# A hybrid decoder layer: the delta rule's chunk matrices stored 64 columns wide, the first stage's units in another order, and the last expert's weights in single transfers

## Chip, cores and metric

The kernel is written in Bass and runs on one core of a Trainium2 chip. The metric is device time in microseconds (us); lower is better. TensorE is called PE, VectorE DVE, ScalarE ACT, GpSimd POOL and SyncE SP.

## What is computed

One layer over 256 tokens of width 1024, in float32. A token mixer has three branches (a gated delta rule with 4 heads of 128, a short gated convolution, and cross-attention into 256 memory tokens), then comes a mixture of 32 experts, 4 to a token, of inner width 1024. Only the delta rule's part within a chunk of 64 tokens is touched in its arithmetic:

```
decay  = exp(where(causal, g_cum_i - g_cum_j, -inf))          # 64 x 64 for each head and chunk
kk     = where(strict, (k*beta) @ k.T * decay, 0)
u, kc  = solve(kk + I, [v*beta, k*beta*exp(g_cum)])            # unit lower triangular
qk     = q @ k.T * decay
step c:  v_new = u - kc @ S;  o = q_dec @ S + qk @ v_new;  S = S*cd + k_end.T @ v_new
```

## The kernel before, in words

**Units and their order.** `mixer_schedule` (lines 100 to 160) writes out one list of units by hand, and every engine walks through that list in order: a unit is, for instance, ("qkv", n), 128 columns of the input projection (24 products of three split float32r operands, L1159 to L1161), ("km", n) and ("vm", t) the memory's keys and values, ("memT", n) and ("hT", t, j) the turning of memory and of the normalised tokens, ("ab", 0) and ("abT", 0) the eight columns of decay and beta, and ("g", name) a step of the delta rule. Units take three PSUM banks in turn (0 to 2): PE waits until the bank of three units ago is free. Weights arrive in slots of 2 MB and are split in pieces (`prep`): ACT rounds the high part (L1035), DVE or POOL subtracts it for the low part (L738). Piece q+3 comes ahead of the unit that uses piece q, and ACT waits for the end of the use of piece q before it writes piece q+3. `vm` takes pieces 4 to 7 (`project_rows`, both tiles of tokens in one run of products), `qkv` n takes piece 8+n.

**The delta rule.** Two chunks of 64 tokens lie on the 128 partitions of a tile, so there are 8 pairs p of tile and head (NPB = 8). Before, each of the matrices LT, LTs, T1, X, XT and decayT is 128x128 for a pair, with only the two diagonal 64x64 blocks other than zero. The steps `scores`, `lx0`, and from n = 1 to 5 `lx n` and `xlx n` build the inverse of the triangular matrix level by level; `xlx` 1 to 4 have two sets of eight products, `xlx5` one. POOL cuts the level's part out of LT by a mask (L978), ACT copies T1 (L466), DVE subtracts (L668 to L683). `kcum`, then `vnew c` and `state c` for the chunks c = 0 to 3, go over the chunks. Between two steps of the delta rule stands mostly one projection unit.

**Masks.** POOL writes the constants at the start (`masks`, L935 to L959) and only then its first low part (L738).

**Experts.** Each expert has 6 chunks of 2 MB: four of gate and up, two of down. They go to a ring of 10 slots. From expert 7 on SP sends the gate and up chunks in pairs of 4 MB (L882 to L894); a pair waits until both slots are free, and signals once. `chunk_spent` is SP's wait for PE's use.

**Barriers.** `ln` at line 1537 waits for tokens and for both LayerNorm parameters before the first statistics.

## Time and profile before

| | |
|---|---|
| median of 3 runs (lowest, highest) | 1306.23 us (1304.66, 1307.99) |
| the profiled execution's own time | 1307.05 us |
| its span, first to last instruction | 1305.3 us |
| mean granted clock of PE, share of full speed | 0.988 |
| bytes moved by DMA | 453.59 MB, 347 GB/s over the span |

The profile comes from one execution; its own time is 1.75 us longer than its span. A row of a timeline gives the start from the beginning of the span, the length, the engine and line, the operation, what it writes and reads, its shape and how many instructions are merged in the row; in brackets stands for how long the engine was idle before and what ended that. PEld is PE's weight load. A float32 product is issued as two instructions, so that "x16" on PE is 8 products. A form such as 128*64 is the part of the array that the weights take, rows and columns: 64*64 is a quarter of it. L numbers are lines of the kernel before.

### The profile page before, as it was taken

What the parts mean: (1) busy time and instruction counts of PE and PEld (TensorE: products, weight loads), DVE (VectorE), ACT (ScalarE), POOL (GpSimd) and SP (SyncE); (2) the same over time, 40 slices, a digit from 0 to 9 for tenths busy, and PEclk for the clock granted to TensorE, in tenths of its full rate; (3) what the DMA queues carried; (4) which work ended last, traced back from release to release, by engine and by line L of the source; (5) the groups of instructions that cost most, each with busy time, mean ns of one, the idle gap of its engine ahead of it and who ended that gap; (6) DMA issues with size and microseconds to landing.
All of it is one profiled execution on the core that took longest, in us unless ns stands there. A gap on an engine that the chain in (4) does not pass through costs nothing.

```text
span 1305.3 us, 16418 instructions
## 1 busy us (share of the span) xinstructions
PE 1236.5 (95%) x6871; PEld 631.9 (48%) x6871; DVE 403.7 (31%) x794; ACT 241.5 (18%) x387; POOL 146.4 (11%) x102
## 2 busy tenths in 40 slices
PE   5899999999999999999999999999999999999996
PEld 5699899899763333333333333333333333323332
DVE  5484563333541222212212212221212222121214
ACT  4453344344321000000000001000000000000001
POOL 6232432355400000000000000000000000000000
PEclk9899999999999999999999999999999999999998
DMA  9443231195499999999999999999999999999993
GB/s 309 141 169 130 79 116 66 65 382 207 160 388 423 398 418 428 424 429 429 430 427 429 433 430 430 431 431 433 426 428 430 433 432 427 430 429 432 427 428 142
DMA packets 49222, 453.59 MB, mean 347 GB/s; under 512 B 6078, under 2 KB 10251, under 8 KB 30987
## 3 DMA queue, kind: packets, MB, share of 16 engines
q1 hardware_dynamic: 49162, 452.71, 83.8%
q8 instruction: 49, 0.80, 0.3%
q14 instruction: 11, 0.08, 0.0%
HBM read 451.64 MB, written 1.05 MB: 347 GB/s over the span
## 4 chain that ended last, share of the span: by engine, by line
PE 70%; DMA 22%; DVE 4%; ACT 2%; issue 1%; SPq 1%; POOL 0%; DVEq 0%; ACTq 0%
PE bank L1339 25%; DMA late<-in_w_gate_up_dram 16%; PE bank L1412 12%; PE bank L1159 6%; PE bank L1160 5%; PE bank L1161 5%; DMA raw<-in_w_gate_up_dram 5%; PE bank L1425 3%; PE bank L1310 3%; PE bank L1325 2%; PE bank L1400 1%; ACT late L1131 1%; PE bank L549 1%; PE bank L554 1%; DMA early<-in_ln_b_dram 1%
## 5 line engine op out<-in xcount | busy, mean ns | idle before, releaser
L1339 PE MATMUL bank<-late 128*64 128x512 f32 x1632 | 366.6, 596 | 14.3 <-DMA late<-in_w_gate_up_dram 14.3
L1339 PEld LDWEIGHTS bank<-late 128*64 128x64 f32 x1632 | 112.0, 137 | 245.8 <-issue 213.8
L1412 PE MATMUL bank<-late 128*64 128x512 f32 x816 | 182.5, 599 | 5.3 <-ACT late L1131 5.3
L1159 PE MATMUL bank<-act_hi,w_hi 128*128 128x256 f32 x448 | 129.6, 289 | 1.7 <-DVE early L1610 1.3
L1160 PE MATMUL bank<-act_lo,w_hi 128*128 128x256 f32 x448 | 126.6, 283 | 0.0
L1161 PE MATMUL bank<-act_hi,w_lo 128*128 128x256 f32 x448 | 126.4, 282 | 0.0
L1753 DVE TENSOR_SCALAR late<-bank 128x512 f32<-128x512 f32 x32 | 22.1, 692 | 308.5 <-PE bank L1339 308.5
L1412 PEld LDWEIGHTS bank<-late 128*64 128x64 f32 x816 | 56.9, 138 | 112.8 <-issue 104.4
L1339 PE MATMUL bank<-raw,late 128*64 128x512 f32 x416 | 93.4, 596 | 3.5 <-DMA raw<-in_w_gate_up_dram 3.5
L738 POOL TENSOR_TENSOR w_lo<-raw,w_hi 128x1024 fp32r<-128x1024 f32 x33 | 80.4, 2438 | 131.7 <-ACT w_hi L1035 131.6
L1159 PEld LDWEIGHTS bank<-act_hi,w_hi 128*128 128x128 f32 x448 | 85.1, 190 | 3.4 <-DVE early L1610 1.5
L1160 PEld LDWEIGHTS bank<-act_lo,w_hi 128*128 128x128 f32 x448 | 85.2, 190 | 0.1
L1161 PEld LDWEIGHTS bank<-act_hi,w_lo 128*128 128x128 f32 x448 | 85.2, 190 | 0.0
L1764 DVE COPY late<-bank 64x512 f32<-64x512 f32 x32 | 22.2, 694 | 190.0 <-PE bank L1412 190.0
L1124 ACT COPY late<-bank 128x512 f32<-128x512 f32 x33 | 19.3, 586 | 332.5 <-PE bank L1310 332.5
L1035 ACT CAST w_hi<-raw 128x1024 fp32r<-128x1024 f32 x56 | 58.5, 1047 | 80.8 <-issue 54.0
L1425 PE MATMUL bank<-late 64*128 64x512 f32 x256 | 63.6, 615 | 1.0 <-DVE late L1824 1.0
L1310 PE MATMUL bank<-hx,late 128*64 128x512 f32 x264 | 62.3, 593 | 0.0
L1133 ACT COPY late<-bank 64x512 f32<-64x512 f32 x32 | 18.5, 579 | 232.0 <-PE bank L1412 232.0
L1339 PEld LDWEIGHTS bank<-raw,late 128*64 128x64 f32 x416 | 28.6, 137 | 62.8 <-issue 55.8
L1129 ACT ACTIVATE late<-late 128x512 f32<-128x512 f32 x32 | 20.1, 629 | 182.7 <-DVE late L1753 182.7
L1768 DVE COPY late<-bank 128x256 f32<-128x256 f32 x31 | 13.2, 425 | 131.2 <-PE bank L1420 131.2
(318 smaller groups left out, 1306.1 us busy)
## 6 DMA issues: line engine op xcount, KB each, us to landing
late<-in_w_gate_up_dram SPq DMA_DIRECT2D x40, 4096.0 KB, 32.5
late<-in_w_down_dram SPq DMA_DIRECT2D x51, 2048.0 KB, 31.1
late<-in_w_gate_up_dram SPq DMA_DIRECT2D x22, 2048.0 KB, 13.4
raw<-in_w_gate_up_dram SPq DMA_DIRECT2D x10, 4096.0 KB, 32.6
raw<-in_w_down_dram SPq DMA_DIRECT2D x13, 2048.0 KB, 33.1
raw<-in_w_in_dram SPq DMA_DIRECT2D x8, 2048.0 KB, 8.4
early<-in_w_in_dram SPq DMA_DIRECT2D x6, 2048.0 KB, 7.9
raw<-in_w_gate_up_dram SPq DMA_DIRECT2D x6, 2048.0 KB, 10.3
```

Source lines behind the costliest of these rows:

```text
L738: ops.tensor_tensor(lo, src, as_f32(hi), ALU.subtract).then_inc(split_lo[who], 1)
L1035: a.copy(hi, src).then_inc(split_hi, 1)
L1159: mm(o, l_hi, r_hi, start=start, stop=False)
L1160: mm(o, l_hi, r_lo, start=False, stop=False)
L1161: return mm(o, l_lo, r_hi, start=False, stop=stop)
L1310: ins = mm(ps[0][64 * c:64 * c + 64, :], onehot[:, t, :], hx[:, t, 512 * c:512 * (c + 1)], start=(t == 0), stop=(t == NT - 1))
L1325: mm(ps[1 + n][64 * c:64 * c + 64, :], e_row[rows, :], bgu[rows, :], start=True, stop=False)
L1339: ins = mm(bk[64 * c:64 * c + 64, :], x_slotT[:, k % 4, 64 * (k // 4):64 * (k // 4) + 64], w[:, kk, at + 512 * c:at + 512 * (c + 1)], star ...
L1412: ins = mm(ps[3][64 * c:64 * c + 64, :], hidT[:, kk, 64 * q:64 * q + 64], w[:, kk, c * 512:(c + 1) * 512], start=(q == 0 and kk == 0), sto ...
L1425: ins = mm(ps[4 + 2 * t + c][:, :], scatter[64 * c:64 * c + 64, t * P:(t + 1) * P], y_tok[64 * c:64 * c + 64, :], start=False, stop=True, ...
L1753: d.tensor_scalar(gate1, ps[1][:, :], LIMIT, None, ALU.min).then_inc(gate_cut, 1)
L1764: d.tensor_copy(y_tok[64:128, :], ps[3][64:128, :]).then_inc(y_copied, 1)
```

## The change

The matrices of the delta rule are stored as two stacked 64x64 blocks, 64 columns wide (`T1`, `LTs`, `X`, `XT`, new `LTc` and `decayTc`). Each product of a pair becomes two, one for each 64 rows (`CHUNK_ROWS`); those of `lx` and `xlx` read partitions 0 to 63 or 64 to 127 and write the same partitions of one bank. `lx0` is now a product with the identity in place of a transpose, `norms` multiplies by 128 columns of ones in place of one, and ACT reads its results from four banks. The copies of ACT, DVE and POOL on these matrices cover half the columns. In the list of units, `vm` now stands between the turns of token tile 0 and of tile 1, `ab`, `abT` and `log decay` stand among the `qkv` units, and `decay` between qkv 9 and 10. The turn of the small parameters (`cols`) is a step of its own, between km 2 and 3. POOL gets four more copies at the end of the masks. The first LayerNorm's statistics no longer wait for its parameters. SP sends the last expert's gate and up chunks one by one. The diff, its context left out (`out_c(b, rows, p)` is the slice `ps[b][rows, p*64:(p+1)*64]`):

```diff
@@ -104,11 +104,11 @@
-    order += [("km", 0), ("ln", 0, 1), ("km", 1), ("km", 2), ("km", 3)]
-    order += [("hT", t, j) for t in range(NT) for j in range(2)] + [("ab", 0), ("abT", 0), ("log decay",)]
-    order += [("vm", n) for n in range(NT)]
-    order += [("g", "scalars"), ("qkv", 0), ("qkv", 1), ("g", "decay"), ("qkv", 2)]
-    order += [("qkv", n) for n in range(3, 12)]
+    order += [("km", 0), ("ln", 0, 1), ("km", 1), ("km", 2), ("cols",), ("km", 3)]
+    order += [("hT", 0, j) for j in range(2)] + [("vm", n) for n in range(NT)] + [("hT", 1, j) for j in range(2)]
+    order += [("qkv", 0), ("qkv", 1), ("ab", 0), ("qkv", 2), ("abT", 0), ("qkv", 3), ("log decay",)]
+    order += [("qkv", n) for n in range(4, 8)] + [("g", "scalars"), ("qkv", 8), ("qkv", 9), ("g", "decay")]
+    order += [("qkv", 10), ("qkv", 11)]
...
@@ -238,7 +238,7 @@
-        T1, LTs = e.at(o_pad, NPB, P), [e.at(o_pad + R, NPB, P), e.at(o_pad + 2 * R, NPB, P)]
+        T1, LTs = e.at(o_pad, NPB, CHUNK), [e.at(o_pad + R, NPB, CHUNK), e.at(o_pad + 2 * R, NPB, CHUNK)]
...
@@ -258,7 +258,7 @@
-        o_x = e.used; X, XT = e.new(NPB, P), e.new(NPB, P)
+        o_x = e.used; X, XT, LTc, decayTc = (e.new(NPB, CHUNK) for _ in range(4))
...
@@ -268,7 +268,9 @@
-        w_ab, ab_rows = e.at(o_qkv + R, KD, 2 * H), e.at(o_qkv, T)
+        w_ab, ab_rows = e.at(o_qkv + R, KD, 2 * H), e.at(o_eb, T)
+        chunk_ident = sb("chunk_ident", [P, CHUNK], scope=early)
+        chunk_mask = sb("chunk_mask", [P, LEVELS, CHUNK], BF16, early)
...
@@ -450,8 +455,11 @@
-                a.activation(inv_norm.rearrange("p t h -> p (t h)"), ps[4][:, 0:2 * NPB], ACT.Sqrt,
-                             bias=eps_rms[:, 0:1]).then_inc(g_act, 1)
+                for t in range(NT):
+                    for n in range(2):
+                        ins = a.activation(inv_norm[:, t, 4 * n:4 * n + 4], ps[4 + 2 * t + n][:, 0::P], ACT.Sqrt,
+                                           bias=eps_rms[:, 0:1])
+                ins.then_inc(g_act, 1)
...
@@ -462,13 +470,12 @@
-                for n in range(2):
-                    ins = a.copy(T1[:, H * n:H * n + H, :].rearrange("p a b -> p (a b)"), ps[4 + n][:, :])
-                ins.then_inc(g_act, 1)
+                a.copy(T1.rearrange("p a b -> p (a b)"), ps[4][:, :]).then_inc(g_act, 1)
-                for n in range(2):
-                    ins = a.mul(nkcT_of(n), ps[4 + n][:, :].rearrange("p (a b) -> p a b", b=P), -1.0)
+                for s, rows in enumerate(CHUNK_ROWS):
+                    ins = a.mul(nkcT.rearrange("p h (t n) -> p t h n", t=NT)[:, :, :, rows],
+                                ps[4 + s][:, :].rearrange("p (t h n) -> p t h n", t=NT, h=H), -1.0)
...
@@ -516,8 +523,7 @@
-                        ins = mm(ps[4][:, t * 2 * H + n:t * 2 * H + n + 1], squares[:, n, t * P:(t + 1) * P], ones[:, 0:1],
-                                 start=True, stop=True)
+                        ins = mm(out4(t * 2 * H + n), squares[:, n, t * P:(t + 1) * P], ones[:], start=True, stop=True)
...
@@ -528,9 +534,11 @@
-                    mm(out4(p), chunk_T(kT, p), chunk_T(kT, p), start=True, stop=True)
+                    for rows in CHUNK_ROWS:
+                        mm(out_c(4, rows, p), chunk_T(kT, p)[:, rows], chunk_T(kT, p)[:, rows], start=True, stop=True)
-                    ins = mm(out4(NPB + p), chunk_T(kT, p), chunk_T(qT, p), start=True, stop=True)
+                    for rows in CHUNK_ROWS:
+                        ins = mm(out_c(6, rows, p), chunk_T(kT, p)[:, rows], chunk_T(qT, p)[:, rows], start=True, stop=True)
...
@@ -543,22 +551,24 @@
-                    if n == 0:
-                        ins = tr(out4(p), LTs[0][:, p, :], ident[:])
-                    else:
-                        ins = mm(out4(p), LTs[n % 2][:, p, :], X[:, p, :], start=True, stop=True)
+                    for rows in CHUNK_ROWS:
+                        ins = mm(out_c(4, rows, p), LTs[n % 2][rows, p, :], ident[rows, rows] if n == 0 else X[rows, p, :],
+                                 start=True, stop=True)
-                    ins = mm(out4(p), T1[:, p, :], XT[:, p, :], start=True, stop=True)
+                    for rows in CHUNK_ROWS:
+                        ins = mm(out_c(4, rows, p), T1[rows, p, :], XT[rows, p, :], start=True, stop=True)
-                        ins = mm(out4(NPB + p), XT[:, p, :], T1[:, p, :], start=True, stop=True)
+                        for rows in CHUNK_ROWS:
+                            ins = mm(out_c(6, rows, p), XT[rows, p, :], T1[rows, p, :], start=True, stop=True)
-                    ins = mm(out4(p), kbe[:, p, :], XT[:, p, :], start=True, stop=True)
+                    for s, rows in enumerate(CHUNK_ROWS):
+                        ins = mm(out_c(4 + s, slice(0, P), p), kbe[rows, p, :], XT[rows, p, :], start=True, stop=True)
...
@@ -567,7 +577,8 @@
-                    ins = mm(o, XT[:, t * H + h, lo:lo + CHUNK], vbeta[:, t * H + h, :], start=True, stop=(c == 0))
+                    rows = CHUNK_ROWS[c % 2]
+                    ins = mm(o, XT[rows, t * H + h, :], vbeta[rows, t * H + h, :], start=True, stop=(c == 0))
...
@@ -637,13 +648,12 @@
-                step(d.tensor_tensor(LT, LT, decayT, ALU.mult))
-                for n in range(2):
-                    o = flat(LT[:, H * n:H * n + H, :])
-                    step(d.tensor_tensor(o, o, ps[4 + n][:, :], ALU.mult))
-                for n in range(2):
-                    o = flat(decayT[:, H * n:H * n + H, :])
-                    step(d.tensor_tensor(o, o, ps[6 + n][:, :], ALU.mult))
+                for rows in CHUNK_ROWS:
+                    step(d.tensor_tensor(LTc[rows], LT[rows, :, rows], ps[4][rows, :].rearrange("p (a n) -> p a n", a=NPB), ALU.mult))
+                for rows in CHUNK_ROWS:
+                    step(d.tensor_tensor(LTc[rows], LTc[rows], decayT[rows, :, rows], ALU.mult))
+                for rows in CHUNK_ROWS:
+                    d.tensor_tensor(decayTc[rows], decayT[rows, :, rows], ps[6][rows, :].rearrange("p (a n) -> p a n", a=NPB), ALU.mult)
...
@@ -667,20 +677,13 @@
-                for n in range(2):
-                    ins = d.tensor_tensor(X[:, H * n:H * n + H, :], ident_8[:, 0:H, :],
-                                          ps[4 + n][:, :].rearrange("p (a n) -> p a n", a=H), ALU.subtract)
-                ins.then_inc(g_dve, 1)
+                d.tensor_tensor(X, ident_8, ps[4][:, :].rearrange("p (a n) -> p a n", a=NPB), ALU.subtract).then_inc(g_dve, 1)
-                for n in range(2):
-                    o = flat(XT[:, H * n:H * n + H, :])
-                    ins = d.tensor_tensor(o, o, ps[4 + n][:, :], ALU.subtract)
+                ins = d.tensor_tensor(flat(XT), flat(XT), ps[4][:, :], ALU.subtract)
-                    for n in range(2):
-                        o = flat(X[:, H * n:H * n + H, :])
-                        ins = d.tensor_tensor(o, o, ps[6 + n][:, :], ALU.subtract)
+                    ins = d.tensor_tensor(flat(X), flat(X), ps[6][:, :], ALU.subtract)
...
@@ -786,7 +789,7 @@
-            return m < PAIRED_FROM or m % 2 == 0 or m % EC == EC - 1
+            return m < PAIRED_FROM or m >= (NE - 1) * EC or m % 2 == 0 or m % EC == EC - 1
...
@@ -879,7 +882,7 @@
-            with sp.Fori(1, ROUNDS) as j:
+            with sp.Fori(1, ROUNDS - 1) as j:
@@ -892,6 +895,18 @@
+            for ex in range(2 + ROUND * (ROUNDS - 1), NE):
+                paired = ex < NE - 1
+                for c in range(EC):
+                    m = EC * ex + c
+                    if c < 4 and paired:
+                        if c % 2 == 0:
+                            chunk_spent(sp, m + 2 - RING)
+                            pair_dma(sp, c, w_gate_up[0, ex], m)
+                    else:
+                        chunk_spent(sp, m + 1 - RING)
+                        chunk_dma(sp, c, w_gate_up[0, ex], w_down[0, ex], *ring_place(m)[0:2])
...
@@ -956,7 +971,14 @@
+                step(ins)
+                for rows in CHUNK_ROWS:
+                    step(eng.tensor_copy(chunk_ident[rows, :], ident[rows, rows]))
+                    ins = eng.tensor_copy(chunk_mask[rows, :, :], level_mask[rows, :, rows])
+                    if rows.start == 0:
+                        step(ins)
+                pool.wait_ge(consts, 3)
...
@@ -974,8 +996,8 @@
-                    m = level_mask[:, n:n + 1, :].broadcast_to([P, NPB, P])
-                    eng.tensor_tensor(LTs[n % 2], LT, m, ALU.mult).then_inc(g_pool, 1)
+                    m = chunk_mask[:, n:n + 1, :].broadcast_to([P, NPB, CHUNK])
+                    eng.tensor_tensor(LTs[n % 2], LTc, m, ALU.mult).then_inc(g_pool, 1)
...
@@ -1207,6 +1229,9 @@
+                if kind == "cols":
+                    pe.wait_ge(rows_in, 80)
+                    tr(ps[3][:, 0:N_ROWS], small_rows[:, :], ident[0:N_ROWS, 0:N_ROWS]).then_inc(cols_turned, 1)
@@ -1237,8 +1262,6 @@
-                    pe.wait_ge(rows_in, 80)
-                    tr(ps[3][:, 0:N_ROWS], small_rows[:, :], ident[0:N_ROWS, 0:N_ROWS]).then_inc(cols_turned, 1)
...
@@ -1251,6 +1274,8 @@
+                    if s == ("qkv", 0):
+                        wait_copied(pe, "hT", 4)
...
@@ -1536,10 +1561,10 @@
-                            v.wait_ge(lnp_in[0], 32)
+                        v.wait_ge(lnp_in[0], 32)
```

## Rows read from the trace of the kernel before

**Rows 1.** The page, busy time of each engine over the whole span.
```profile
PE 1236.5 (95%) x6871; PEld 631.9 (48%) x6871; DVE 403.7 (31%) x794; ACT 241.5 (18%) x387; POOL 146.4 (11%) x102
```
**Rows 2.** Busy time by stretch: engines, granted clock, share of DMA time, GB/s.
```profile
28.10:55.60 27.50, 19.41 (x92) 14.31 (x93) 13.87 (x22) 12.57 (x19) 7.97 (x3) 0.81 0.46 165
...
32.40:42.60 10.20, 5.14 (x24) 3.34 (x25) 5.46 (x8) 2.46 (x3) 1.41 (x1) 0.50 0.47 173
...
107.40:110.90 3.50, 3.50 (x18) 3.50 (x18) 0.25 (x1) 0.28 (x1) 0.00 (x0) 0.51 0.73 275
...
135.00:205.30 70.30, 66.59 (x557) 65.43 (x556) 42.64 (x70) 27.34 (x50) 26.42 (x12) 1.00 0.25 91
...
254.00:382.00 128.00, 124.07 (x918) 115.83 (x916) 60.21 (x130) 52.37 (x80) 54.28 (x30) 0.97 0.68 261
382.00:830.00 448.00, 442.84 (x2104) 151.60 (x2102) 100.32 (x208) 39.37 (x65) 0.00 (x0) 1.00 1.00 424
830.00:1260.00 430.00, 409.00 (x1952) 139.75 (x1950) 94.93 (x202) 35.13 (x59) 0.00 (x0) 1.00 1.00 430
```
**Rows 3.** Timeline of TensorE, first stage: start, length, instructions, idle time before and its releaser.
```profile
20.92 0.36 PE L1159 MATMUL bank<-src_hi,w_hi 128*128 128x256 f32 x1 [1.29 <-POOL w_lo L738]
...
35.99 1.12 PE L1237 MATMUL bank<-ident,hx 128*128 128x128 f32 x4 [3.61 <-DVE act_lo L1601]
...
44.28 0.50 PE L1159 MATMUL bank<-w_hi,src_hi 128*128 128x512 f32 x1
...
55.58 0.28 PE L504 MATMUL bank<-tiny,block_upper 128*128 128x8 f32 x2
```
**Rows 4.** The same timeline for GpSimd, ScalarE and VectorE, first stage.
```profile
13.70 3.15 POOL L955 TENSOR_TENSOR level_mask<-early 128x128 bf16<-128x128 f32 x6
...
18.40 2.37 POOL L738 TENSOR_TENSOR w_lo<-raw,w_hi 128x1024 fp32r<-128x1024 f32 x1
...
27.04 1.05 ACT L1035 CAST w_hi<-raw 128x1024 fp32r<-128x1024 f32 x1 [0.26 <-DMA raw<-in_w_mem_kv_dram]
...
47.38 1.28 ACT L1059 ACT_TABLE_LOAD   x1
...
56.78 1.07 ACT L1047 COPY early<-bank 128x512 f32<-128x512 f32 x2
...
37.76 0.69 DVE L1601 TENSOR_TENSOR act_lo<-bank,act_hi 128x512 fp32r<-128x512 f32 x1 [0.64 <-ACT act_hi L1040]
```
**Rows 5.** The chain of waits, the delta rule's steps: start, length, what.
```profile
103.96 3.46 PE bank L519 x32
...
146.89 1.78 PE bank L554 x16
```
**Rows 6.** Timeline of TensorE, the same stage: two steps that found it waiting.
```profile
136.15 1.09 PE L547 MATMUL bank<-ident,early 128*128 128x128 f32 x8 [1.08 <-POOL early L978]
...
142.04 2.02 PE L549 MATMUL bank<-early 128*128 128x128 f32 x16 [1.97 <-issue]
```
**Rows 7.** Timeline of the weight loads, steps over the chunks: one pair of loads a row.
```profile
216.36 0.25 PEld L570 LDWEIGHTS bank<-early 128*64 128x64 f32 x2
216.58 0.25 PEld L572 LDWEIGHTS bank<-early 128*64 128x64 f32 x2
...
221.34 0.19 PEld L583 LDWEIGHTS bank<-early 128*64 128x64 f32 x2 [0.17 <-issue]
221.70 0.19 PEld L584 LDWEIGHTS bank<-early 64*64 64x64 f32 x2 [0.17 <-issue]
```
**Rows 8.** Timeline of the weight loads, an expert's biases and what follows them.
```profile
409.84 0.21 PEld L1325 LDWEIGHTS bank<-late 32*64 32x64 f32 x8 [0.81 <-issue]
410.86 0.14 PEld L1339 LDWEIGHTS bank<-late 128*64 128x64 f32 x2 [0.81 <-issue]
```
**Rows 9.** Timeline of TensorE, the last expert's first products by each pair of chunks.
```profile
1262.92 3.65 PE L1339 MATMUL bank<-late 128*64 128x512 f32 x16 [1.03 <-DMA late<-in_w_gate_up_dram]
...
1273.69 7.09 PE L1339 MATMUL bank<-late 128*64 128x512 f32 x32 [1.45 <-DMA late<-in_w_gate_up_dram]
```

More of the change, by code:

```diff
@@ L163 @@
 SCHEDULE, PIECES_OF = mixer_schedule()
-NOT_UNITS = ("g", "prep", "ln", "ya", "sum hi", "sum", "soft", "log decay")
+NOT_UNITS = ("g", "prep", "ln", "ya", "sum hi", "sum", "soft", "log decay", "cols")
 UNITS = [s for s in SCHEDULE if s[0] not in NOT_UNITS]
@@ L438, in hybrid_layer @@
             GD[name] = gd
+        CHUNK_ROWS = [slice(CHUNK * n, CHUNK * (n + 1)) for n in range(P // CHUNK)]
         def act_gdn(act, name):
@@ L480, in act_gdn @@
                 a.activation(o_rs, o_ss, ACT.Sqrt, bias=eps_rms[:, 0:1], scale=1.0 / DH).then_inc(g_act, 1)
-        def nkcT_of(t):
-            return nkcT[:, :, t * P:(t + 1) * P]
         def pt4(h):
@@ L495, in spread, with out_c @@
                 return a[:, t, n:n + 1].broadcast_to([P, P])
+            def out_c(b, rows, p):
+                return ps[b][rows, p * CHUNK:(p + 1) * CHUNK]
             def chunk_T(a, p):
@@ L583, in pe_gdn @@
                         mm(o, qT[:, h, t * P + lo:t * P + lo + CHUNK], state[:, h, :], start=True, stop=False)
-                    mm(o, decayT[rows, t * H + h, rows], vnew[rows, h, :], start=(c == 0), stop=True)
+                    mm(o, decayTc[rows, t * H + h, :], vnew[rows, h, :], start=(c == 0), stop=True)
                 for h in range(H):
@@ L601, in flat @@
                 return a.rearrange("p a b -> p (a b)")
-            ident_8 = ident[:].rearrange("p (a n) -> p a n", a=1).broadcast_to([P, NPB, P])
+            ident_8 = chunk_ident[:].rearrange("p (a n) -> p a n", a=1).broadcast_to([P, NPB, CHUNK])
             if name == "scalars":
@@ L1577, in _ @@
                                     ALU.subtract).then_inc(bank_free[bank_of(u)], 1)
+                    continue
+                if kind == "cols":
+                    v.wait_ge(cols_turned, 1)
+                    d.tensor_copy(small_cols[:], ps[3][:, 0:N_ROWS]).then_inc(cols_ready, 1)
+                    v.wait_ge(cols_ready, 1)
                     continue
@@ L1618, in _ @@
                 elif kind == "ab":
-                    v.wait_ge(cols_turned, 1)
-                    d.tensor_copy(small_cols[:], ps[3][:, 0:N_ROWS]).then_inc(cols_ready, 1)
-                    v.wait_ge(cols_ready, 1)
                     full()
```

## Prediction

> **What bounds the kernel now.** The page comes first: PE is busy 95% of the span [rows 1]. Then the stretches. From 382 us on the experts run with DMA at its full share and 424 to 430 GB/s, PE nearly always busy up to 830 us and waiting 21 us of 430 after that [rows 2]: the stream of weights sets the pace there, PE just behind it. Ahead of that DMA is far from full (share 0.68 even in the last stretch of the mixer, 0.25 in the delta rule's) and PE is the bound: 124.07 of 128 us busy, 66.59 of 70.3 [rows 2]. The stream of expert weights starts when the mixer frees its slots, so what the mixer saves on PE should move all that follows. The first stage stands out: from 28.1 to 55.6 us PE is busy 19.41 of 27.5 us, at half clock from 32.4 to 42.6 [rows 2].
>
> All sums are made against the profiled execution's own time, 1307.05 us; the median is 0.8 us lower. About 0.3% (4 us) is what a measurement here can tell from no change.
>
> **First stage.** Before, the last turn of a token tile waits 3.61 us for DVE's queue, `ab` follows at half clock, and `vm` runs only from 44.28 to 55.58, 11.3 us; then qkv 0 starts, 55.9 [rows 3]. After, I lay it out anew:
> - POOL gets five more waits and four copies of 64 rows, two of 64 and two of 384 columns, ahead of its first low part. The nearest row has 0.525 us for 128 columns with two inputs (3.15 for six) [rows 4]: 3.7 us at that price, half of it if a copy with one input costs half. I take 2.6, towards the middle. The low part that ends at 20.77 and releases PE at 20.92 [rows 3, 4] then comes at 23.5; two km units of 24 products at 0.118 us (11.3 us for 48 longer ones is twice that) bring 29.3. The statistics, freed of the parameters, only shorten DVE's side.
> - Two turns end at about 30.5. The high part of piece 4 still starts at 27.04, since its DMA lands then; 1.05 us of ACT and 2.37 of POOL [rows 4] give 30.5 too. `vm` ends at 42.
> - Then a new hole. ACT's order is the copy for piece 10 (which waits for the end of `vm`), both copies of `vm`, then the high parts of token tile 1: 1.05 + 1.07 + two of about 0.6, then DVE's 0.69 [rows 4], 4.0 us. qkv 0 needs all four turns and starts at 46.
> - `ab`, `abT` and `scalars` now stand behind that: 24 products of 0.118 us and 0.5, 3.4 us, so the comparable time is 49.4. ACT's three table loads of 1.28 us each for `abT` [rows 4] had `vm` as cover; now they stand among silus and high parts that are ordered only three pieces ahead. They hold ACT for 4.5 us where two units of 2.85 us less 3.4 us for a piece give slack of 2.3: about 1.7 us of wait, 51.1.
> - Clock: holes of 4 us stand where PE waits for POOL and behind `vm`. It fell once at such a place before; a shorter spell lasted 3.5 us at 0.51 [rows 2], 1.7 us lost. One and a half such losses: 53.6.
>
> Gain 55.9 - 53.6 = **2.3 us**; between -1.5 (both holes cold, POOL at full price) and 5.5 (no cold spell, cheap copies). The moved `decay` has the same neighbours in kind (two qkv units) as before: nothing either way. `cols` on PE is one small turn, and it goes in the wait on the parts of km.
>
> **Norms.** 16 one-column products take 3.46 us [rows 5]; 16 full ones take 3.56 (two sets of 1.78). Behind them the clock was 0.51 for 3.5 us [rows 2], with PE busy all the time, which costs 1.7 us. If columns that work keep it up, that returns; from 0 to 1.7, I take 1.5, as nothing else stands before that fall. ACT's four reads in place of one hide behind a unit.
>
> **The delta rule's products.** A set of eight 128x128 products takes 1.78 us, 0.111 for each of 16 instructions [rows 5]. There are 18 sets: scores 2, lx0 1 (transposes, 0.9 us), lx 5, xlx 9, kcum 1: 17 x 1.78 + 0.9 = 31.2 us. After, each set is 32 instructions of half the columns in weights and in what streams, 0.056 us each. The question is whether the two blocks run side by side. An expert's biases answer it: eight instructions of 512 columns (0.44 us each alone, by 0.111 for 128) in four places of the array take 1.02 us from first load to the next stage's first [rows 8], not 3.6. So a set takes 16 x 0.056 = 0.9. Each change of the array's form costs: pairs of one form follow each other in 0.22 us, pairs of alternating forms in 0.36 [rows 7], 0.145 for a change. Before, these steps had none, after two each (projections are 128*128). Seven single sets 1.19 each, five double (scores, xlx 1 to 4) 2.09, kcum with 128 weight columns 1.78 + 0.29: 8.3 + 10.4 + 2.1 = 20.8. **Gain 10.4 us**; if the blocks don't overlap, none and 5 us of cost (below).
>
> `vnew` 1 to 3 get worse: the product with XT is now 64*64 and the next 128*64, which is just what `state` has; 0.36 in place of 0.22 a pair, 8 pairs, three times: **3.5 us lost**. `vnew0` and `state` stay.
>
> **Waits in that stage.** 66.59 of 70.3 us busy leaves 3.7 idle [rows 2], of which lx0 waits 1.08 for POOL's mask product and lx1 1.97 [rows 6], behind DVE's X. Both operands are halved in columns, each of three copies from over 2 us to about 1.1, while PE's own steps shorten by 0.6 to 1.5 beside units of 2.85. I take 2.8 of the 3.7; bounds 1 and 3.7.
>
> **The last expert.** PE waits 1.03 us for the first pair of chunks and 1.45 for the second [rows 9]. A chunk is half a pair, 4.9 us at 430 GB/s [rows 2]; sent singly the first half lands that much earlier, so both waits go and the second half is there when it is needed: **2.5 us**. Below, 0 if the last down chunks are late instead (they must land by 1285); above, 3.5. SP issues two more transfers, far ahead of a stream 36 us deep, at no cost.
>
> Sum: 2.3 + 1.5 + 10.4 - 3.5 + 2.8 + 2.5 = 16.0. 1307.05 - 16.0 = 1291.0, and 1290.2 for the median.
>
> **A rule against the change.** The biases' first two row tiles write one bank at the same time, in different halves of its partitions, and still all eight end in 1.02 us; one bank at a time would take 1.8 [rows 8]. The Trainium skill, TensorEngine Tiling (Array Packing), section Restrictions and Gotchas, says that "Different row tiles cannot access same PSUM bank simultaneously". By it the blocks of lx and xlx, which share a bank, would run one behind the other, and the sum would be 2.5. The trace disagrees with the rule for different partitions, and the sum goes by the trace.
>
> **Rivals.**
> - *Blocks of one bank take turns*: 64-row blocks might behave otherwise than the biases' 32-row ones. Seven sets cost 0.9 us more and four double ones 1.8: 13.5 us, 1303.7. The page above is the rule for it; rows 8 speak against it. 12%.
> - *A change of place costs like a change of form*, at lx, xlx, scores and kcum: every one of 288 products then stands alone, 0.111 + 0.145 in place of 0.056, 58 us more, 1348. It turns into a loss from 0.056 us a product over the forecast. Rows 8 speak against it (the place changes there at no cost), no row shows it for short products. 4%.
> - *The first stage loses*: POOL's copies at full price, both holes cold, ACT's tables holding pieces back longer: -2 in place of 2.3, 1294.5. For it, the hole behind `vm` is sure; against it, `vm` no longer waits for `ab`. 14%.
> - *The mixer's gain is swallowed by the weights*: if their stream didn't start earlier, only the end's 2.5 us would stay, 1303.7. Against it, share 0.68 ahead of 382 us. 4%.
> - The forecast has 66%, its own range 1284 to 1300 by the bounds above.
>
> The range goes from 1284 to 1304, which takes in the two cases at 1303.7. Faster by over 0.3% is the forecast and the third rival, 0.80; within 0.3% the first and the fourth, 0.14 of their 0.16; slower 0.06, the second and what the others may add.
>
> **What would show it.** Right: lx and xlx sets at 0.9 us with 0.15 idle ahead of them, `vnew` pairs at 0.36 apart, no half clock behind norms, no waits at lx0 and lx1, a hole of 4 us behind `vm`, and no wait ahead of the last expert's third chunk. Wrong: sets at 1.8 us or more (the blocks take turns), qkv 0 later than 49 us, or a mixer that ends 13 us earlier with experts that end less so.

## The result, and the profile after

| | median, us | runs |
|---|---|---|
| kernel before | 1305.89 | 1304.66 to 1307.99 (4) |
| kernel after | 1297.25 | 1295.85 to 1298.25 (4) |

The ratio is 0.9931 with the interval 0.9914 to 0.9949: faster by 8.6 us. The forecast was 16.0 us, 1290.2. The profiled execution of after took 1295.85 us with a span of 1294.0; by the two profiled executions the difference is 11.2 us.

The page of the kernel after, busy time of each engine and the granted clock in 40 slices:

```profile
PE 1226.6 (95%) x7167; PEld 618.8 (48%) x7167; DVE 392.9 (30%) x785; ACT 240.3 (19%) x386; POOL 144.9 (11%) x106
...
PEclk8999999999999999999999999999999999999998
```

PE is 9.9 us less busy than in [rows 1]. Where that went is read from marks that both kernels have. Each row is a start time in the two profiles, from the chain of waits, which has the norms 0.16 us later than TensorE's timeline, and the last column is what the stretch up to it gained (+) or lost (-):

| mark | before | after | stretch |
|---|---|---|---|
| qkv 0 | 55.94 | 50.78 | |
| norms | 103.96 | 108.00 | -4.04 (from the start) |
| scores | 121.14 | 123.66 | +1.5 |
| lx0 | 136.15 | 136.96 | +1.7 |
| vnew0 | 205.56 | 196.73 | +9.6 |
| end of state3 | 252.27 | 246.42 | -3.0 |
| `down` of the expert before the last | 1253.78 | 1245.23 | +2.7 |
| last `down` | 1284.14 | 1272.81 | +2.8 |

Of the 2.7 us between state3 and the experts' end, 1.5 are a spell of half clock at 401 us in the profile of before; after has none there. The medians are 8.64 us apart, 2.7 less than the marks say. That the marks at the end of state3 and at the last expert give 5.85 and 2.8, 8.65 together, fits, but no run shows that the 2.7 us are missing in the other executions.

**The delta rule's products.** The chain of waits of after, its steps from the scores to kcum (start, length, what):

```profile
123.66 1.08 PE bank L538 x32
...
136.96 1.15 PE bank L555 x32
...
145.25 1.08 PE bank L562 x32
...
190.46 1.93 PE bank L571 x32
```

A set that took 1.78 us in 16 instructions [rows 5] now takes 1.08 in 32. The second set of a double step takes 0.93 (146.33 to 147.26), and kcum 1.93. So the two blocks of 64 rows run at the same time although they write one bank. The start times of the single instructions say the same: in the set at 141.14 the two blocks' instructions start 0.007 us apart, and the next two 0.058 us after the first two.

**The steps over the chunks.** The weight loads of after, one pair of loads a row:

```profile
207.15 0.19 PEld L581 LDWEIGHTS bank<-early 64*64 64x64 f32 x2 [0.33 <-issue]
207.51 0.19 PEld L583 LDWEIGHTS bank<-early 128*64 128x64 f32 x2 [0.17 <-issue]
```

The pairs of `vnew` stand 0.36 us apart, as those of `state` did before [rows 7].

**The first stage.** TensorE's timeline of after; in brackets the idle time ahead of the row and its releaser:

```profile
25.46 0.55 PE L1181 MATMUL bank<-src_hi,w_hi 128*128 128x256 f32 x1 [5.60 <-POOL w_lo L741]
...
35.23 0.47 PE L1181 MATMUL bank<-w_hi,src_hi 128*128 128x512 f32 x1 [0.67 <-ACT early L1067]
...
68.19 0.39 PE L1181 MATMUL bank<-act_hi,w_hi 128*128 128x256 f32 x1 [1.15 <-DVE early L1640]
...
76.05 0.36 PE L1181 MATMUL bank<-act_hi,w_hi 128*128 128x256 f32 x1 [1.92 <-POOL w_lo L741]
...
79.40 0.39 PE L1181 MATMUL bank<-act_hi,w_hi 128*128 128x256 f32 x1 [0.28 <-DVE early L1640]
...
107.84 3.73 PE L526 MATMUL bank<-ones,early 128*128 128x128 f32 x32
```

The waits of 1.15, 1.92 and 0.28 us have two causes. ScalarE and VectorE ahead of them:

```profile
63.88 1.05 ACT L1057 CAST w_hi<-raw 128x1024 fp32r<-128x1024 f32 x1 [2.80 <-issue]
...
71.03 1.28 ACT L1081 ACT_TABLE_LOAD   x1
```

```profile
64.97 1.23 DVE L741 TENSOR_TENSOR w_lo<-raw,w_hi 128x1024 fp32r<-128x1024 f32 x1 [2.98 <-ACT w_hi L1057]
66.11 0.48 DVE L1637 TENSOR_SCALAR early<-bank,small_cols 128x256 f32<-128x256 f32 x1
```

The 1.92 and 0.28 us come behind the table loads of `abT` (65.27, 69.51 and 71.03) and the one back to silu (73.49): the high parts that they wait for start only at 72.44 and 75.11. The 1.15 us at 68.19 have no table load ahead of them in their chain. ACT stood idle for 2.80 us before it, since a piece may be overwritten only when PE is done with it; DVE stood behind that high part, read the bank of `qkv` 2 only from 66.11 on, and PE, with the short unit `abT` between, was back at that bank before DVE had read it.

The low part that released PE at 20.92 [rows 3] now does so at 25.46. GpSimd's timeline says why:

```profile
18.48 0.23 POOL L976 COPY chunk_ident<-ident 64x64 f32<-64x64 f32 x1
18.77 0.50 POOL L977 COPY chunk_mask<-level_mask 64x384 bf16<-64x384 bf16 x1
19.33 1.11 POOL L976 COPY chunk_ident<-ident 64x64 f32<-64x64 f32 x1
20.51 1.53 POOL L977 COPY chunk_mask<-level_mask 64x384 bf16<-64x384 bf16 x1
22.12 3.19 POOL L741 TENSOR_TENSOR w_lo<-raw,w_hi 128x1024 fp32r<-128x1024 f32 x1
```

The first two copies take 0.73 us, and the same two for the other rows 2.64; the low part takes 3.19 instead of 2.37 [rows 4]. What differs is the neighbour and not the rows: put off to 110.97 us (experiment 1), the same copies take 1.23 and 0.54 us for the first rows and 0.23 and 0.51 for the others, and there VectorE's low part ends at 112.11. VectorE at the start of after:

```profile
18.84 1.51 DVE L1530 SCALAR_TENSOR_TENSOR hx<-hx,tiny,early 128x1024 f32<-128x1024 f32 x1
20.38 1.28 DVE L1532 SCALAR_TENSOR_TENSOR hx<-hx,tiny,early 128x1024 f32<-128x1024 f32 x1
21.70 1.41 DVE L741 TENSOR_TENSOR w_lo<-raw,w_hi 128x1024 fp32r<-128x1024 f32 x1
```

These read two tensors each and run back to back from 18.84 on. The first of them started at 21.01 in the kernel before; the statistics, rid of the parameters, came early enough to meet POOL's copies.

Busy time by stretch of the kernel after (window, its length, PE, PEld, DVE, ACT, POOL, then granted clock, share of DMA time and GB/s):

```profile
23.60:30.40 6.80, 4.94 (x23) 4.97 (x24) 4.17 (x8) 1.61 (x3) 3.74 (x2) 0.50 1.05 395
...
46.50:50.78 4.28, 1.26 (x9) 0.81 (x8) 1.29 (x2) 2.99 (x5) 2.35 (x1) 1.00 0.29 107
...
50.86:54.28 3.42, 3.42 (x17) 3.42 (x18) 0.00 (x0) 0.00 (x0) 0.00 (x0) 0.50 0.00 0
...
111.50:115.00 3.50, 3.50 (x32) 3.50 (x31) 0.26 (x1) 1.24 (x5) 0.00 (x0) 1.00 1.01 383
...
135.80:196.60 60.80, 58.36 (x824) 55.21 (x822) 34.60 (x60) 25.17 (x46) 21.26 (x12) 1.00 0.30 105
```

The clock is at its lower level, 1.2 GHz, three times before the norms: from 13.30 to 16.70 in the first unit of km (0.50 too, and the wait for POOL covers it), at the third unit of km, behind the wait of 5.60 us, and at qkv 0, behind the hole of 4.28 us. Behind the norms it stays at 2.4 GHz where it had fallen before [rows 2].

**The last expert.** TensorE's timeline of after:

```profile
1253.26 3.65 PE L1364 MATMUL bank<-late 128*64 128x512 f32 x16
...
1262.41 7.04 PE L1364 MATMUL bank<-late 128*64 128x512 f32 x32
...
1272.81 7.09 PE L1437 MATMUL bank<-raw,late 128*64 128x512 f32 x32 [0.27 <-ACT late L1153]
```

Nothing waits for a chunk of `gate_up` any more, where 1.03 and 1.45 us stood [rows 9].

### The profile page after: what moved, and what is told of

It reads as the page before. It is cut to its first block, busy times and chain, and to the rows that moved or that the text cites. A ratio compares the mean times of both kernels' runs of the same rounds, so it can differ in the third digit from the quotient of the medians.

```text
span 1294.0 us, 16946 instructions
## 1 busy us (share of the span) xinstructions
PE 1226.6 (95%) x7167; PEld 618.8 (48%) x7167; DVE 392.9 (30%) x785; ACT 240.3 (19%) x386; POOL 144.9 (11%) x106
## 4 chain that ended last, share of the span: by engine, by line
PE 69%; DMA 21%; DVE 3%; ACT 2%; issue 1%; POOL 0%; SPq 0%; DVEq 0%; ACTq 0%
PE bank L1364 25%; DMA late<-in_w_gate_up_dram 21%; PE bank L1437 12%; PE bank L1181 6%; PE bank L1182 5%; PE bank L1183 5%; PE bank L1450 3%; PE bank L1335 3%; PE bank L1350 2%; PE bank L1425 1%; ACT late L1153 1%; ACT w_hi L1057 1%; PE bank L1445 1%; PE bank L555 1%; PE bank L562 0%
## 6 DMA issues: line engine op xcount, KB each, us to landing
late<-in_w_down_dram SPq DMA_DIRECT2D x51, 2048.0 KB, 31.3
```

## The experiments

All times are medians, each beside runs of the kernel before on the same chip (1306 to 1308 us). The ratios come from all the runs, not from the two medians, so they differ a little from those medians' quotient. A difference from the kernel after is one of medians and crosses chips; differences under 2 us between two variants are not told apart here.

**1. POOL's copies put off.** The four copies go out of the start and run at the norms.

```
-                for rows in CHUNK_ROWS:
-                    step(eng.tensor_copy(chunk_ident[rows, :], ident[rows, rows]))
-                    ins = eng.tensor_copy(chunk_mask[rows, :, :], level_mask[rows, :, rows])
...
+                if s == ("g", "norms"):
+                    for rows in CHUNK_ROWS:
+                        step(eng.tensor_copy(chunk_ident[rows, :], ident[rows, rows]))
+                        step(eng.tensor_copy(chunk_mask[rows, :, :], level_mask[rows, :, rows]))
```

> The changed kernel with one thing moved: GpSimd's four new copies (the two diagonal blocks of the identity and of the level masks) stand at the norms step instead of at the end of the masks, so that its first low part of a weight piece comes as early as before. Nothing is left out. My theory: in the changed kernel those copies and the low part behind them, slowed by VectorE's two-input work, end at 25.4 us where before they ended at 20.8, and TensorE waits 5.6 us for them. Moved away, km 2 starts at about 21 us, vm at about 31 us instead of 35.2, and the whole gains 4 us: 1293 us, with the hole at 20 us down to about 1.3 us. Rival: vm is tied to the landing and split of its own pieces (the high part of piece 4 starts at 27.2 us in either kernel), so the hole only moves to before vm: gain under 1.5 us, 1296 or more.

Measured: 1296.85 us (1296.16 to 1298.31), ratio 0.9918 (0.989 to 0.9947). No gain over after. The copies did hold up km, whose third unit now starts at 21.20 instead of 25.46 and its fourth at 24.57 instead of 30.61, and all that came back was lost ten microseconds later: the norms start at 108.79, where after has 107.84. TensorE, VectorE and GpSimd of this kernel:

```profile
36.04 0.77 PE L1180 MATMUL bank<-w_hi,src_hi 128*128 128x512 f32 x1 [2.85 <-DVE act_lo L1630]
```

```profile
27.96 1.28 DVE L1531 SCALAR_TENSOR_TENSOR hx<-hx,tiny,early 128x1024 f32<-128x1024 f32 x1
29.28 2.23 DVE L1570 CAST w_ab_hi<-early 128x64 fp32r<-128x64 f32 x1
31.62 2.26 DVE L1571 TENSOR_TENSOR w_ab_lo<-early,w_ab_hi 128x64 fp32r<-128x64 f32 x1
33.80 1.21 DVE L741 TENSOR_TENSOR w_lo<-raw,w_hi 128x1024 fp32r<-128x1024 f32 x1
```

```profile
28.54 5.25 POOL L741 TENSOR_TENSOR w_lo<-raw,w_hi 128x1024 fp32r<-128x1024 f32 x2 [7.78 <-ACT w_hi L1056]
```

The split of `ab`'s 64 columns takes 0.20 us an operation in the kernel after, where POOL is idle at that time:

```profile
27.96 0.20 DVE L1571 CAST w_ab_hi<-early 128x64 fp32r<-128x64 f32 x1
```

Here it takes 2.23 and 2.26 while POOL works through two low parts, and `vm` waits for a low part of h queued behind it.

**2. The old order of the first stage**, the rest of the change kept: all four turns, `ab`, `vm`, qkv 0.

> The changed kernel with the order of units of the kernel before from hT on (both token tiles' turns, ab, abT and log decay ahead of vm, scalars and decay among the first qkv units). The new copies stay in their early place. Nothing is left out. My theory: the new order costs, it does not gain, since it opens a hole of 4 us behind vm and takes away the cover of ScalarE's three table loads; with the old order and the earlier statistics the turns end at about 36 us, vm at 52.5, norms starts at about 100 instead of 108, and the time is 1290 us. Rival: the new order saves the 8 us of half-idle TensorE that the old one has ahead of vm, and the lateness comes from the copies alone: 1300 us or more.

Measured: 1291.97 us (1290.02 to 1292.76), ratio 0.9878 (0.9849 to 0.9908), 5.3 us better than after. The norms start at 102.75 instead of 107.84. The new order costs about what TensorE's timeline says of the norms, 5.1 us, less than the 7 us expected. The wait for POOL's low part is still there (4.55 us at 25.57): it is not the order's.

**3. Both together.**

> Both edits together: old order of units and the four copies moved to the norms step. Nothing is left out. My theory: the two add up nearly; turns end at about 31 us, vm runs from 35 to 46.5, norms starts at about 95 us, the time is 1285 us (1283 to 1288). Rival: one hole covers the other, and it is no faster than the better of the two alone.

Measured: 1293.55 us (1292.02 to 1296.57), ratio 0.9899 (0.9867 to 0.9931). No better than the old order alone: the two operations of the split took 2.24 and 2.29 us, a turn waited 3.13 for DVE, and the clock was at half for 13.65 us from 30.8 on.

**4. The blocks apart.** All upper blocks of a set are issued before all lower ones; the work is the same. One of the five loops:

```
-                for p in range(NPB):
-                    for rows in CHUNK_ROWS:
+                for rows in CHUNK_ROWS:
+                    for p in range(NPB):
                         ins = mm(out_c(4, rows, p), T1[rows, p, :], XT[rows, p, :], start=True, stop=True)
```

> The changed kernel with the loops over pair and block exchanged in scores, lx and xlx: all eight products of partitions 0 to 63 first, then all eight of partitions 64 to 127. The same products, nothing is left out. My theory: two blocks overlap only when neighbours in the queue use different places of the array; apart, a set takes 32 x 0.056 = 1.8 us instead of the 0.93 to 1.08 measured, and 16 sets cost 0.8 us more each, less what lies in waits: 1308 to 1311 us. Rival: TensorE's queue looks far enough ahead, or starts the second block's products while the first block's run, and the set stays at about 1 us: 1297 us.

Measured: 1306.99 us (1304.83 to 1309.9, ten runs), ratio 1.0001 (0.9986 to 1.0016): 9.7 us above after, 1 us less than expected. Its chain of waits:

```profile
138.42 1.87 PE bank L555 x32
143.32 1.82 PE bank L555 x32
```

and its costliest groups between 120 and 210 us (count, busy time, mean ns of one, idle time before), with the same group of after below:

```profile
L555 PE MATMUL bank<-early 64*64 64x64 f32 x160 | 9.5, 221 | 0.0
```

```profile
L555 PE MATMUL bank<-early 64*64 64x64 f32 x160 | 5.7, 221 | 0.8 <-issue 0.8
```

One product takes 221 ns from start to end in both, and only the overlap differs. Two products' instructions side by side in the queue and in different places take 0.058 us together; instructions for one place behind each other start 0.058 us apart each, and the whole gain of the change is gone.

**5. Products grouped by form.** `vnew` and `state` issue all 64\*64 products of a chunk, then all 128\*64 ones. Each head's first product keeps its start mark. The Trainium skill, PSUM — Partial Sum Buffer, section The four PSUM rules, says that a second group's start in the same bank and rows makes the first group's next product overwrite its sum; so this kernel leaves the first part of the sums of heads 0 to 2 out of its output. It issues the same instructions.

```
                 for h in range(H):
...
-                    if c:
-                        ins = mm(o, nkcT[:, h, t * P + lo:t * P + lo + CHUNK], state[:, h, :], start=False, stop=True)
+                for h in range(H if c else 0):
+                    ins = mm(ps[6][rows, h * DH:(h + 1) * DH], nkcT[:, h, t * P + lo:t * P + lo + CHUNK], state[:, h, :],
+                             start=False, stop=True, skip_group_check=True)
```

> The changed kernel with the products of vnew and state regrouped: in vnew first the four heads' products with XT (64*64 part of the array), then the four with the state (128*64), in state first the four with the queries (128*64), then the four with decayTc (64*64); the sums in PSUM are the same. Nothing is left out. My theory: each change of the form costs 0.145 us and has no cover, so 6 changes fewer in each of six steps give 36 x 0.145 = 5.2 us: 1292 us, with rows of pairs 0.22 us apart. Rival: the gap between the forms is a gap for the weight load of another product and comes back elsewhere in the step: no more than 1 us.

Measured: 1291.46 us (1290.6 to 1293.66), ratio 0.9885 (0.986 to 0.9911), 5.8 us below after. The weight loads of `vnew` in this kernel:

```profile
206.28 0.84 PEld L580 LDWEIGHTS bank<-early 64*64 64x64 f32 x8 [0.33 <-issue]
207.29 0.85 PEld L583 LDWEIGHTS bank<-early 128*64 128x64 f32 x8 [0.17 <-issue]
```

Eight loads of one form, then one change, where after has a change for every two. `vnew` and `state` of three chunks had 7 changes each inside them and keep one: 36 fewer, by 0.145 us 5.2 us.

**6. One column for the norms**, as before, the rest kept.

```
-ins = mm(out4(t * 2 * H + n), squares[:, n, t * P:(t + 1) * P], ones[:], start=True, stop=True)
+ins = mm(out4(t * 2 * H + n)[:, 0:1], squares[:, n, t * P:(t + 1) * P], ones[:, 0:1], start=True, stop=True)
```

> The changed kernel with norms' 16 products back to one column of ones (into the first column of the same slices, which ScalarE reads anyway). Nothing is left out. My theory: 3.5 us of one-column products let the granted clock fall to half behind them, as in the kernel before at 107.4 us, and cost 1.7 us: 1299 us, with a stretch of half clock within 4 us of norms' end. Rival: the fall before was chance, no stretch at half clock follows norms, and the time stays at 1297.

Measured: 1296.14 us (1295.97 to 1297.8), ratio 0.992 (0.9896 to 0.9945). The half clock is back right behind the norms, with PE busy throughout:

```profile
112.50:115.90 3.40, 3.40 (x19) 3.40 (x18) 0.25 (x1) 0.00 (x0) 0.00 (x0) 0.51 0.80 301
```

The 1.7 us don't show in the median, 1.1 below after's. They are less than these runs tell apart, and the profile of after had a spell at 330.8 us that this one had not. In all three profiles with one-column norms (before, 6 and 7) such a spell stands behind them, and in none of the eleven with 128 columns. That is shown, and what it is worth in the end is not.

**7. The last expert's chunks singly, on the kernel before.**

> The kernel before with one part of the change alone: the last expert's gate and up chunks are sent one by one, each with a signal of its own. Nothing is left out. My theory: TensorE's waits of 1.03 and 1.45 us ahead of the last expert's pairs go, and all of it reaches the end: 2.5 to 2.8 us, 1303.3 us. Rival: the last down chunks become the bound, or the weights' stream ends later for the smaller transfers: under 1 us.

Measured: 1304.12 us (1302.57 to 1306.28, ten runs), ratio 0.9977 (0.9965 to 0.9988): 2.6 us, as the forecast had it.

**8. The split of `ab` behind the last turn's low part**, added to experiment 1: its two operations move from between token tile 1's LayerNorm and the low parts of h to behind the last of those.

```
                     d.tensor_tensor(lo, src, as_f32(hi), ALU.subtract).then_inc(free, 1)
+                    if s == ("hT", 1, 1):
+                        v.wait_ge(ab_in, 16)
+                        step(d.tensor_copy(w_ab_hi[:], w_ab))
+                        d.tensor_tensor(w_ab_lo[:], w_ab, as_f32(w_ab_hi[:]), ALU.subtract).then_inc(ab_split, 2)
```

> The changed kernel with two things moved: GpSimd's four copies to the norms step (as in e1) and VectorE's split of the eight decay and beta columns' weights from behind the first LayerNorm to behind the low parts of token tile 1. Nothing is left out. My theory: in e1 the gain of the earlier km units was lost in VectorE's queue, where the two small operations of the split took 2.23 and 2.26 us instead of 0.2 and 0.23 each, because GpSimd's two low parts ran back to back at that time and held the port that both engines share; vm then waited 2.85 us for token tile 0's low part. With the split moved that wait goes, and the time is 3 to 4 us under e1: 1293 us. Rival: the next operation in the queue, the low part of piece 5, takes the split's place behind GpSimd and vm waits as long: 1297 us.

Measured: 1294.45 us (1291.41 to 1297.22), ratio 0.991 (0.9884 to 0.9936). The wait in `vm` shrank from 2.85 to 0.40:

```profile
33.80 0.47 PE L1180 MATMUL bank<-w_hi,src_hi 128*128 128x512 f32 x1 [0.40 <-DVE act_lo L1626]
```

and qkv 0 starts at 47.94, 2.8 us before after's. The medians of experiments 1 and 8 differ by 2.4 us with overlapping runs, on different chips; in the two profiles the norms start at 108.79 and 103.46. The wait is shown, the gain of the whole probable.

**9. All turns, then `vm`, then `ab`**, on top of experiment 8.

```
+    order += [("hT", t, j) for t in range(NT) for j in range(2)] + [("vm", n) for n in range(NT)]
+    order += [("ab", 0), ("abT", 0), ("log decay",)]
+    order += [("g", "scalars"), ("qkv", 0), ("qkv", 1), ("g", "decay"), ("qkv", 2)]
```

> On the changed kernel: the order all four turns of the token tiles, vm, ab, abT, log decay, scalars, qkv 0 and on (decay behind qkv 1), with the two moves of e10 (GpSimd's copies at norms, the split of the small weights behind the turns). Nothing is left out. My theory: the first stage loses by holes at three places, ahead of vm, behind vm, and where ScalarE's three table loads stand among the silus; here the high and low parts of both tiles are ready before vm's run ends, and the table loads fall in the first three qkv units, ahead of which pieces are split already. vm should start at about 31 to 32 us and run to 43, norms at about 95 to 96 us instead of 108 (108.8 in e1), 6 to 8 us under e10: 1287 us. Rival: vm waits as long for the third low part as qkv 0 did behind it, and the table loads hold the pieces back here too: 1293 us or more.

Measured: 1297.5 us (1294.36 to 1297.8), ratio 0.9922 (0.9896 to 0.9947). A miss:

```profile
56.70 0.60 PE L511 MATMUL bank<-tiny,block_upper 128*128 128x8 f32 x2 [5.13 <-DVE tiny L1579]
```

The scalars need the log decay, which comes behind ACT's three table loads (50.03, 53.08 and 54.60, 1.28 us each), and here no unit of products stood between. The clock then stayed at half for 10.2 us.

**10. The same, with the products grouped**, the start mark on the first head alone, so that every sum is whole.

> e8 with the products of vnew and state grouped by form as in e5, the start mark on the first head's product alone (in e5 each head's product carried it, which left the sums of three heads without their first part). Nothing is left out. My theory: the two gains are in different stages and both on TensorE's path, so they add: e8 less 5 to 6 us, 1281 to 1282 us. Rival: the weights' stream holds part of the gain back at the end: 1284 or more.

Measured: 1292.3 us (1290.37 to 1294.46), ratio 0.9882 (0.9859 to 0.9906): 5.2 us below experiment 9 on the same chip. Grouping adds to the rest.

**11. `ab` ahead of qkv 0**, the one edit on the kernel after.

```
-    order += [("qkv", 0), ("qkv", 1), ("ab", 0), ("qkv", 2), ("abT", 0), ("qkv", 3), ("log decay",)]
+    order += [("ab", 0), ("abT", 0), ("log decay",), ("qkv", 0), ("qkv", 1), ("qkv", 2), ("qkv", 3)]
```

> The changed kernel with one part of its new order undone: ab, abT and log decay stand ahead of qkv 0, behind the turns of token tile 1, instead of among qkv 1 to 4. Nothing is left out. My theory: TensorE's waits of 1.15, 1.92 and 0.28 us between 66 and 80 us come from ScalarE's three table loads (1.28 us each) and VectorE's wait for them, standing where the pieces are split just in time; ahead of qkv 0 three pieces are ready already, and 2 to 3 us come back: 1294.5 us. Rival: the loads hold piece 11 back there as they did piece 13, and the time stays at 1297.

Measured: 1293.77 us (1293.45 to 1295.28), ratio 0.9892 (0.9866 to 0.9917), some 3.5 us below after. The waits of 1.15, 1.92 and 0.28 us are gone, and the norms start at 104.31 instead of 107.84. ACT's table loads now fall while it owes PE nothing, and `abT` no longer stands between two units of qkv. The run doesn't part these two.

**12. What the runs point to**: turns, `vm`, `ab`, `abT`, log decay, then eight units of qkv before the scalars; the copies and the split late; the products grouped.

```
+    order += [("hT", t, j) for t in range(NT) for j in range(2)] + [("vm", n) for n in range(NT)]
+    order += [("ab", 0), ("abT", 0), ("log decay",)] + [("qkv", n) for n in range(8)]
+    order += [("g", "scalars"), ("qkv", 8), ("qkv", 9), ("g", "decay"), ("qkv", 10), ("qkv", 11)]
```

> e11 with scalars and decay of the delta rule back where the changed kernel has them, behind qkv 7 and qkv 9. Nothing is left out. My theory: e8 and e11 lost their gain at one place, a wait of 5.13 us at scalars, for which g_log is due only after ScalarE's three table loads, and the half clock of 6.8 to 10.2 us that followed that hole. With seven projection units in between nothing waits for g_log, and norms starts at 99 to 101 us instead of 107.8 (e8) and 108.9 (e11): 7 to 9 us under e11's 1292.3, 1284 to 1285 us. Rival: the table loads hold up the pieces behind qkv 3 instead, and only the clock comes back: 1288 us or more.

Measured: 1282.76 us (1282.1 to 1286.95), ratio 0.9826 (0.9812 to 0.984): 24.3 us below the kernel before and 14.5 below after. TensorE's timeline of this kernel:

```profile
33.48 1.12 PE L1262 MATMUL bank<-ident,hx 128*128 128x128 f32 x4 [2.00 <-DVE act_lo L1627]
...
99.53 3.73 PE L525 MATMUL bank<-ones,early 128*128 128x128 f32 x32
```

The 2.00 us are the longest wait of PE from km's second unit to the norms, the clock is at half once in that stretch (6.8 us at 31.3), and the norms start 8.3 us before those of after. Against experiment 10 only the scalars and the decay stand elsewhere, and the norms start 9.4 us earlier (99.53 against 108.93) and the median is 9.5 lower: a step placed right behind what it needs, with no unit between, costs that much. In experiment 10 it is a wait of 5.13 us and 6.8 us at half clock behind it.

## Why the prediction was right in kind and its gain 7 us too large

- **The delta rule's products: right.** Sets at 1.08 to 1.15 and 0.93 us stood against 1.19 and 0.9; kcum at 1.93 against 2.07. The biases' row [rows 8] carried over from 32 rows to 64. The rule that the prediction quotes from the Trainium skill, TensorEngine Tiling (Array Packing), section Restrictions and Gotchas, that different row tiles cannot use one bank at the same time, does not hold here for tiles that write different partitions: experiment 4 shows what it costs when they really run one behind the other, 1.82 us a set and 9.7 in all. That run also shows a condition that I had not stated: the overlap is between neighbours in the queue.
- **`vnew`: right**, 3.0 us against 3.5. The term counted 8 changes a chunk and there were 7; 7 x 0.145 x 3 is 3.04. Experiments 5 and 10 confirm the price by taking it away.
- **Norms: right** by the profile (no half clock behind them, 1.5 us gained), and not resolved by medians (experiment 6).
- **Waits in the delta rule's stage: too high.** The stretch from before lx0 to `vnew0` had 3.7 us idle [rows 2], and 60.80 less 58.36, 2.4, are left: 1.3 gained, not 2.8. lx0 still waits 0.80 us for POOL's mask product, halved in columns but not in the operations ahead of it.
- **The last expert: right**, 2.8 us in the profile and 2.6 alone, against 2.5.
- **First stage: the step that failed.** It was to bring the norms 2.3 us earlier and they came 4.04 later, a miss of 6.3 us. qkv 0 started at 50.78, past the 49 us that the prediction had named as a sign of being wrong. By its own steps:
  - "POOL gets five more waits and four copies": taken at 2.6 us, was 4.5 (20.92 to 25.46). The bound of 3.7 came from rows of POOL alone, and none of them had a neighbour that reads two tensors. "The statistics, freed of the parameters, only shorten DVE's side" was wrong: they moved DVE's operations with two inputs onto POOL's copies. +2.0 with the start of km's unit.
  - From there to `vm` 7.0 us were forecast and 9.77 passed. 4.9 us of it, from 25.5 to 30.4, ran at half clock, 2.5 us lost. With the 1.7 lost at qkv 0 the clock cost 4.2, against 2.5: +1.7. Where the falls would stand was right (behind the wait for POOL and behind `vm`), and the first lasted twice as long.
  - The hole behind `vm` came as forecast, 4.28 us for 4.0: +0.3.
  - `ab` and `abT` among the qkv units: 1.15 + 1.92 + 0.28, 3.35 us of wait against 1.7: +1.65. The table loads alone are 2.20, 0.5 more than forecast; the 1.15 us at the bank behind the short unit `abT` stood in no term. Experiment 11 took all of it away by order alone.
  - 2.0 + 1.7 + 0.3 + 1.65 is 5.65; 0.65 us are spread over the rest and not explained.

  The rival "the first stage loses" described this: copies at full price or more, both holes cold, tables that hold pieces back. Its own sum was -2, still 2 us short, and it had 14%. By the marks the terms fell short by 6.3 us in the first stage, 1.5 in the waits and 0.4 in the products, less 0.5 at `vnew` and 0.3 at the last expert: 7.4 us, as much as the medians lack. The profiles lack only 4.7, for they have 2.7 us between state3 and the last expert that no term forecast.

POOL's late start and the order don't add up as separate faults. Moving the copies alone brought nothing (experiments 1 and 3), since the same two engines then met over `ab`'s split. With the split moved too `vm` ran through early, and the norms came 4.4 us before those of after (experiment 8). With `ab` behind `vm` and the scalars behind eight units of qkv it was 8.3 us (experiment 12).

## What to carry to other kernels

A product on a quarter of the array is worth its half columns only if its neighbour in the queue uses another place and the same form: alternate places, group forms, and count the changes. When setup work moves to another engine, price it beside what runs there at that moment, not by the row of that engine alone; if it holds the first product of a chain, put it where nobody waits. Before a rare operation with a table load is moved in a just-in-time order, find which queue it shares with the pieces that PE needs next. A unit much shorter than its neighbours covers nothing and still takes its turn in the ring of banks.

## What was not expected of the hardware

- VectorE and GpSimd hold each other up for whole operations: a cast of 64 columns took 0.20 us alone and 2.23 beside POOL's two low parts back to back; copies on POOL took 0.23 and 0.50 us alone and 1.11 and 1.53 beside DVE's operations with two inputs; a low part of 1024 columns took 3.19 instead of 2.37. The Trainium skill, Advanced Engine Details and Errata, section VectorE Performance Modes, says that GpSimd's instructions and VectorE's "2p" ones block each other. The rows agree that the two engines block each other; they don't say which of VectorE's ran as "2p", and those beside POOL's copies had two tensor inputs. They put a price on it that the small operation's own length says nothing of.
- The clock fell behind 3.5 us in which PE was busy all the time with one-column products (experiments 6 and 7, and [rows 2]), and did not with 128 columns for the same weights.
- A change of form in the array costs 0.145 us (5.2 us for 36 of them by that price, 5.8 and 5.2 measured in experiments 5 and 10), and a change of place shows none: alternating places, each pair of instructions still starts 0.058 us after the last.
